# Turning x by a diagonal of reciprocal roots at the start of a gated hybrid attention layer

## What is computed

```python
def rmsnorm(x, g):
    xf = x.astype(jnp.float32)
    y = xf * lax.rsqrt(jnp.mean(xf * xf, axis=-1, keepdims=True) + RMS_EPS)
    return (y * g.astype(jnp.float32)).astype(x.dtype)

def hybrid_layer(x, norm_g, w_in, b_merge, w_pa, w_pb, w_out):
    h = rmsnorm(x, norm_g)
    proj = jnp.einsum('bsd,dc->bsc', h, w_in)
    # ... attention branches, gates and merge, all from proj
```

## Time and profile before

| | us |
|---|---|
| median of three runs | 443.52 (443.51 to 444.15) |
| profiled execution, its own time | 443.48 |
| its span, first to last instruction | 441.7 |
| TensorE busy | 431.6 (98%) |
| VectorE busy | 212.8 (48%) |
| ScalarE busy | 198.5 (45%) |
| GpSimd busy | 176.3 (40%) |

### The profile page before, as it was taken

One profiled execution on the slowest core, in us unless ns is written; L12 is line 12 of the kernel. 1 busy time (PEld: TensorE's weight loads), 2 busy tenths in 40 slices (PEclk: granted clock), 3 DMA queues, 4 the chain that ended last, 5 costly groups with the idle time before them and its releaser, 6 DMA issues.

```text
span 441.7 us, 6258 instructions
## 1 busy us (share of the span) xinstructions
PE 431.6 (98%) x2377; PEld 374.5 (85%) x2377; DVE 212.8 (48%) x367; ACT 198.5 (45%) x401; POOL 176.3 (40%) x113
## 2 busy tenths in 40 slices
PE   7899999999999999999999999999999999999995
PEld 6789998899889988988888888888888888888885
DVE  3831244344435446757857664827025173083334
ACT  5743555335544464567555554533223543332111
POOL 4744442243243333646499543534355354200000
PEclk9999999999999999999999999999999999999999
DMA  8962234622452263024122022222222284210421
GB/s 284 286 192 96 96 96 83 159 96 95 91 150 97 96 168 110 25 96 143 49 95 96 0 73 96 96 72 96 95 71 96 95 261 156 113 66 0 149 90 47
DMA packets 40044, 48.31 MB, mean 109 GB/s; under 512 B 3768, under 2 KB 35536, under 8 KB 40016
## 3 DMA queue, kind: packets, MB, share of 16 engines
q1 hardware_dynamic: 37568, 47.72, 34.4%
q10 hardware_dynamic: 2448, 0.21, 0.4%
HBM read 39.48 MB, written 2.15 MB: 94 GB/s over the span
## 4 chain that ended last, share of the span: by engine, by line
PE 96%; DMA 2%; DVE 1%; ACT 1%; SPq 0%; issue 0%; DVEq 0%; ACTq 0%
PE ps L766 20%; PE ps L770 20%; PE ps L767 20%; PE ps L816 4%; PE ps L818 4%; PE ps L817 4%; PE ps L890 3%; PE ps L974 3%; PE ps L975 3%; PE ps L973 3%; PE ps L873 3%; PE ps L917 3%; PE ps L907 2%; DMA xs<-in_x 2%; PE ps L865 1%; PE ps L850 0%
## 5 line engine op out<-in xcount | busy, mean ns | idle before, releaser
L662 POOL TENSOR_TENSOR w_lo<-raw,w_hi 128x1024 fp32r<-128x1024 f32 (+1 forms) x59 | 138.1, 2342 | 175.4 <-ACT w_hi L990 175.4
L766 PE MATMUL ps<-hT_hi,w_hi 128*128 128x512 f32 x336 | 135.0, 402 | 1.1 <-DVE hT_lo L1241 1.1
L770 PE MATMUL ps<-hT_lo,w_hi 128*128 128x512 f32 x336 | 131.2, 390 | 0.0
L767 PE MATMUL ps<-hT_hi,w_lo 128*128 128x512 f32 x336 | 131.1, 390 | 0.0
L770 PEld LDWEIGHTS ps<-hT_lo,w_hi 128*128 128x128 f32 x336 | 63.1, 188 | 13.5
L766 PEld LDWEIGHTS ps<-hT_hi,w_hi 128*128 128x128 f32 x336 | 63.2, 188 | 11.2 <-issue 1.3
L767 PEld LDWEIGHTS ps<-hT_hi,w_lo 128*128 128x128 f32 x336 | 63.3, 188 | 9.9
L990 ACT CAST w_hi<-raw 128x1024 fp32r<-128x1024 f32 (+1 forms) x58 | 59.2, 1020 | 8.3 <-PE ps L770 5.4
L816 PE MATMUL ps<-w_hi,hT_hi 128*128 128x256 f32 x160 | 45.6, 285 | 0.0
L818 PE MATMUL ps<-w_lo,hT_hi 128*128 128x256 f32 x160 | 44.7, 279 | 0.0
L817 PE MATMUL ps<-w_hi,hT_lo 128*128 128x256 f32 x160 | 44.6, 279 | 0.0
(11 more groups left out here) (148 smaller groups left out, 665.6 us busy)
## 6 DMA issues: line engine op xcount, KB each, us to landing
raw<-in_w_in SPq DMA_DIRECT2D x25, 1024.0 KB, 4.9
KTs<-KTs SPq DMA_DIRECT2D x20, 256.0 KB, 3.4
raw<-in_w_out SPq DMA_DIRECT2D x4, 1024.0 KB, 4.8
xs<-in_x SPq DMA_DIRECT2D x4, 512.0 KB, 5.3
raw<-in_w_pb SPq DMA_DIRECT2D x4, 512.0 KB, 4.1
res<-in_x SPq DMA_DIRECT2D x4, 512.0 KB, 3.9
out<-weighted SPq DMA_DIRECT2D x8, 256.0 KB, 2.1
raw<-in_w_in SPq DMA_DIRECT2D x2, 512.0 KB, 8.9
```

Of the source, the lines that this page charges most:

```text
L662: nc.gpsimd.tensor_tensor(ring(w_lo, n, kt), src, ring(w_hi, n, kt).bitcast(F32), ALU.subtract).then_inc(lo_ready, 1)
L766: pe.matmul(out, wh, hh, start=(k == 0), stop=False)
L767: pe.matmul(out, wl, hh, start=False, stop=False)
L770: return pe.matmul(out, wh, hl, start=False, stop=(k == kts - 1))
```

## The change

- x is not scaled any more. Per tile ScalarE squares the low half of the rows and VectorE the high half, VectorE makes `ss_mean`, ScalarE takes the root of both together (`rms`, kept in `var`), VectorE its reciprocal, and the identity times that reciprocal is a diagonal `diag[:, i, :]`. VectorE makes the diagonals of tiles 0 to 2, ScalarE that of tile 3.
- TensorE multiplies each block of x by the diagonal (`pe.matmul` with the block as the stationary operand), which turns and scales it at once. It was `pe.transpose` before.
- The vectors are turned right behind the warm-up, ahead of tile 0. VectorE copies them out behind tile 0's diagonal and ahead of tile 1's square.
- Of tile 2 six blocks are turned; the last two alternate with the first blocks of tile 3.
- The first half of the first weight chunk is loaded as two DMAs (k 0 to 3, k 4 to 7), with a semaphore each.
- POOL builds the distance tables behind the low part of step 2, and VectorE finishes the constants behind step 2's results.

```diff
 # sync
-                        sp.dma_start(dst[:, :, 0:P], w_in_t[:, :, at:at + P]).then_inc(first_half_in[0], 16)
-                        sp.dma_start(dst[:, :, P:256], w_in_t[:, :, at + P:at + 256]).then_inc(first_half_in[1], 16)
+                        for m, ks in enumerate((slice(0, FIRST_K), slice(FIRST_K, KT_D))):
+                            sp.dma_start(dst[:, ks, 0:P], w_in_t[:, ks, at:at + P]).then_inc(first_in[m], 16)
+                        sp.dma_start(dst[:, :, P:256], w_in_t[:, :, at + P:at + 256]).then_inc(first_in[2], 16)
 # gpsimd: iota and affine_select of d_full, d_band, d_quad, d_hex go into distances()
-            pool.wait_ge(first_half_in[0], 16)
+            pool.wait_ge(first_in[0], 16)
             nc.gpsimd.tensor_copy(hi[:, low_k, :], src[:, low_k, :]).then_inc(first_hi, 1)
+            pool.wait_ge(first_in[1], 16)
             nc.gpsimd.tensor_copy(hi[:, high_k, :], src[:, high_k, :]).then_inc(hi_ready, 1)
...
                 lows(n)
+                if n == CONST_STEP:
+                    distances()
 # tensor
-            for i in range(TT):
-                if i < HALVED:
-                    pe.wait_ge(x_scaled, i + 1)
-                else:
-                    pe.wait_ge(x_scaled_low, i - HALVED + 1)
...
-                    last = pe.transpose(ps[:, k, P * i:P * i + P], xs[:, i, P * k:P * k + P], ident[:, :])
...
+            pe.wait_ge(vec_in, 32)
+            pe.transpose(ps[:, 7, SEQ - 24:SEQ], vecs[:, :], ident[0:24, 0:24]).then_inc(vecs_turned, 1)
+            def scaled_turn(i, k):
+
+                return pe.matmul(ps[:, k, P * i:P * i + P], xs[:, i, P * k:P * k + P], diag[:, i, :],
+                                 start=True, stop=True)
+
+            for i in range(TT - 1):
+                pe.wait_ge(diag_ready, i + 1)
+                for k in range(KT_D if i < TT - 2 else FIRST_TURNS):
+                    if i == 0 and k == KT_D - 1:
+                        pe.wait_ge(gb_ready, 1)
+                    scaled_turn(i, k)
+            pe.wait_ge(last_diag, 1)
+            for k in range(KT_D):
+                scaled_turn(TT - 1, k).then_inc(x_turned, 1)
+                if FIRST_TURNS + k < KT_D:
+                    scaled_turn(TT - 2, FIRST_TURNS + k)
 # scalar
+            for i in range(TT):
+                low = slice(0, D // 2)
                 act.wait_ge(x_in[i], 16)
-                nc.scalar.activation(squares[:, i, 0:n], xs[:, i, 0:n], ACT.Square,
+                nc.scalar.activation(squares[:, i, low], xs[:, i, low], ACT.Square,
                                      accum_out=ss[:, i:i + 1]).then_inc(squared, 1)
...
+                act.wait_ge(squared, i + 1)
+                act.wait_ge(part_ready, i + 1)
+                nc.scalar.activation(var[:, i:i + 1], ss[:, i:i + 1], ACT.Sqrt, scale=1.0 / D,
+                                     bias=ss_mean[:, i:i + 1]).then_inc(rms_ready, 1)
+            act.wait_ge(last_root, 1)
+            nc.scalar.activation(diag[:, TT - 1, :], ident[:, :], ACT.Copy,
+                                 scale=rstd[:, TT - 1:TT]).then_inc(last_diag, 1)
 # vector
+            def square_rows(i):
+                high = slice(D // 2, D)
+                dve.wait_ge(x_in[i], 16)
+                link(nc.vector.scalar_tensor_tensor(out=squares[:, i, high], in0=xs[:, i, high], scalar=1.0,
+                                                    in1=xs[:, i, high], op0=ALU.mult, op1=ALU.mult,
+                                                    accum_out=ss_part[:, i:i + 1]))
+                nc.vector.tensor_scalar(ss_mean[:, i:i + 1], ss_part[:, i:i + 1], 1.0 / D, EPS, ALU.mult,
+                                        ALU.add).then_inc(part_ready, 1)
+
+            def root_diagonal(i):
+                dve.wait_ge(rms_ready, i + 1)
+                if i == TT - 1:
+                    nc.vector.reciprocal(rstd[:, i:i + 1], var[:, i:i + 1]).then_inc(last_root, 1)
+                    return
+                link(nc.vector.reciprocal(rstd[:, i:i + 1], var[:, i:i + 1]))
+                nc.vector.tensor_scalar(diag[:, i, :], ident[:, :], rstd[:, i:i + 1], None,
+                                        ALU.mult).then_inc(diag_ready, 1)
+
+            dve.wait_ge(consts_ready, 1)
+            for i in range(TT):
+                square_rows(i)
+                root_diagonal(i)
+                if i == 0:
+                    dve.wait_ge(vecs_turned, 1)
+                    link(nc.vector.tensor_copy(gb[:], ps[:, 7, SEQ - 24:SEQ]))
+                    nc.vector.tensor_scalar(hbias[:], gb[:, 8:24], 0.5, None, ALU.mult).then_inc(gb_ready, 1)
...
                 if s:
                     take_step(s - 1)
+                if s == CONST_STEP + 1:
+                    finish_constants()
```

More of the change, by code:

```diff
@@ L87 @@
 FIRST_K = 4
-HALVED = 2
+FIRST_TURNS = 6
 WARM = 14
 NRING = 4
+CONST_STEP = 2
 SKEW = 8
@@ L390, in hybrid_layer_program @@
         raw_in = [sem(f"raw_in{i}") for i in range(NRAW)]
-        first_half_in = [sem(f"first_half_in{i}") for i in range(2)]
+        first_in = [sem(f"first_in{i}") for i in range(3)]
         const_step = sem("const_step")
@@ L396, in hybrid_layer_program @@
         dve_chain = sem("dve_chain")
[L397 to L400, removed]
+        part_ready = sem("part_ready")
+        rms_ready = sem("rms_ready")
+        diag_ready = sem("diag_ready")
+        last_root = sem("last_root")
+        last_diag = sem("last_diag")
         first_hi = sem("first_hi")
@@ L738, in _ @@
                 pe.matmul(ps[:, 0, 0:P], ident[:, :], ident[:, :], start=True, stop=True)
-            for i in range(TT):
-                if i < HALVED:
-                    pe.wait_ge(x_scaled, i + 1)
-                else:
-                    pe.wait_ge(x_scaled_low, i - HALVED + 1)
-                for k in range(KT_D):
-                    if i >= HALVED and k == KT_D // 2:
-                        pe.wait_ge(x_scaled, i + 1)
-                    if i == 1 and k == 7:
-                        pe.wait_ge(gb_ready, 1)
-                    last = pe.transpose(ps[:, k, P * i:P * i + P], xs[:, i, P * k:P * k + P], ident[:, :])
-                    if i == TT - 1:
-                        last.then_inc(x_turned, 1)
-                if i == 0:
-                    pe.wait_ge(vec_in, 32)
-                    pe.transpose(ps[:, 7, SEQ - 24:SEQ], vecs[:, :], ident[0:24, 0:24]).then_inc(vecs_turned, 1)
+            pe.wait_ge(vec_in, 32)
[7 more added lines that the diff above has]
+                    if i == 0 and k == KT_D - 1:
+                        pe.wait_ge(gb_ready, 1)
+                    scaled_turn(i, k)
[4 more added lines that the diff above has]
+                    scaled_turn(TT - 2, FIRST_TURNS + k)
             def weights_wait(n):
@@ L1208, in turn_vectors @@
-            def turn_vectors():
-                dve.wait_ge(vecs_turned, 1)
-                link(nc.vector.tensor_copy(gb[:], ps[:, 7, SEQ - 24:SEQ]))
-                nc.vector.tensor_scalar(hbias[:], gb[:, 8:24], 0.5, None, ALU.mult).then_inc(gb_ready, 1)
-            for i in range(HALVED):
-                variance(i)
-                scale_rows(i, 0)
-            turn_vectors()
-            last, high = TT - 1, slice(D // 2, D)
-            dve.wait_ge(x_in[last], 16)
-            link(nc.vector.scalar_tensor_tensor(out=squares[:, last, high], in0=xs[:, last, high], scalar=1.0,
-                                                in1=xs[:, last, high], op0=ALU.mult, op1=ALU.mult,
-                                                accum_out=ss_part[:, 0:1]))
@@ L1230, in _ @@
-            nc.vector.reciprocal(rvar[:, last:TT], var[:, last:TT]).then_inc(var_ready, 1)
-            for i in range(HALVED, TT):
-                scale_rows(i, D // 2)
+            def square_rows(i):
[6 more added lines that the diff above has]
+                                        ALU.add).then_inc(part_ready, 1)
```

92 lines of the change are left out of this document (30 added, 62 removed).

## The result

The kernel after took 444.65 us (median of 20 executions, 443.40 to 446.99), the kernel before beside it 443.49 (20, 442.96 to 444.55). The ratio is 1.003, with an interval of 1.0019 to 1.0041: slower by 0.3%, where the forecast was 443.65 and no difference. 16 of the 20 lie between 443.4 and 445.1 and four between 446.7 and 447.0. The profiled execution is one of these four: 446.98 us, its span 445.1. The kernel before beside that second set has 443.54. So the medians differ by 1.2 and by 0.5 us, the two intervals together reach from a gain of 0.4 to a loss of 1.8 us, and the first set has a spread of 3.6 us that the prediction didn't expect. The question is what makes the start as long as 18 us, and what is there when it isn't.

The account below looks back on a forecast made before the run. TensorE was taken as the bound, busy 431.6 of 441.7 us, so the time shifts with the first projection matmul (14.58). 443.48 + 0.07 (diagonals and doubled turns) + 0.10 (POOL beside VectorE) = 443.65, range 442.9 to 444.3.

Parts of the forecast that it names:

- Part 2: VectorE's queue stands still until the vectors are turned behind the warm-up, at 6.98; tile 1's square then starts at 7.60.
- Parts 1 and 2: VectorE's queue before the first projection matmul: 1.51 us a tile, last diagonal seen by TensorE at 12.36.
- s1: Start of VectorE's square of tile 1, forecast at 7.60.
- s3: Start of VectorE's square of tile 3, forecast at 10.62.
- Part 4: POOL's first cast beside VectorE's square of tile 3: the square grows by 0 to 0.38, taken as +0.10 us.
- B: Rival: TensorE's clock rises later, so warm-up and tile 0's turns end later; together 444.5 us; chance 0.10.
- Rival A: VectorE's queue holds the tiles back less: 443.1 us, about 442.7 with the clock's rise 1 us earlier; chance 0.17.
- C: Rival: distance tables or constants aren't hidden; at twice their time step 3 waits 1.8 us: 445.4; chance 0.03.
- D: Rival: the last diagonal follows tile 3's landing and TensorE isn't in the way: 442.2 us; chance 0.05.
- The f32 turn as two instructions: TensorE's turns go from 0.11 to 0.224 us each, 32 from 3.6 to 7.2; first projection matmul at 14.65, +0.07.
- Part 5: Distance tables, constants and an additional load issue moved later on POOL, VectorE and SP: cost 0, bounds 0 and +0.3.

Follow-up runs that it names:

- second set: The changed kernel measured again, nothing altered, 12 executions: 444.05 us, ratio 1.0005 (0.9992 to 1.0018).
- r_after: The changed kernel run again unaltered, for a second profile: 444.05 us, ratio 1.0005, first projection matmul at 14.98.
- e4: The changed kernel with POOL's distance tables back in front of its first cast: 444.00 us, ratio 0.9999.
- e3: The changed kernel with the vectors turned behind tile 2's blocks, copied behind the low weights, and POOL's second cast waiting for VectorE's low weights: 445.24 us, ratio 1.0021.
- g1: The kernel before with only the split first weight load and the moved tables and constants; x still scaled and transposed: 444.37 us, ratio 1.0014.
- h3: The changed kernel with transposes by the identity instead of f32 matmuls by the diagonal, scaling of x left out: 444.18 us, ratio 1.0014.
- e2: The changed kernel with POOL waiting for VectorE's low weights before its second cast: 444.52 us, ratio 1.0005.
- h1: The changed kernel with the vectors turned after 9 of the 14 warm-up matmuls: 443.42 us, ratio 0.9994.
- e1: The changed kernel with the vectors turned behind tile 2's blocks and copied behind VectorE's low weights: 443.90 us, ratio 1.0006.
- f1: The changed kernel with 6 warm-up matmuls instead of 14: 443.82 us, ratio 1.0000.
- f2: The changed kernel with 6 warm-up matmuls instead of 14 and POOL's second cast waiting for VectorE's low weights: 443.85 us, ratio 1.0005.

## Why the prediction was wrong, step by step

The forecast had the first matmul at 14.58 + 0.07 + 0.10 = 14.75; the trace of 446.98 us has 18.00. The 3.25 us between them:

- **Part 2, when the queue moves on.** The forecast let the vectors' turn start at 6.98; it came at 7.59, 0.61 later, and at 6.34 in r_after. The mechanism was right, the moment was read from one trace of a quantity that varies: in the profiled executions of the same start the spacing of the instructions falls at moments between 4.6 (e4) and 7.3 (after, e3, g1, h3).
- **Parts 1 and 2, the length of a tile.** Forecast 1.51 us, measured 1.70 (7.92, 9.63, 11.33 in e2, with no long instruction). ScalarE's root with a tile as bias takes 0.30, not the 0.20 of the earlier trace rows. The diagonal takes 0.29, not 0.23: the row that I took it from multiplies by a constant. And the root starts 0.10 behind the mean, not 0.04. The two tiles between s1 and s3 make +0.39. Then the last tile: root +0.10, ScalarE's own diagonal 0.40 for 0.32 and somewhat longer gaps, +0.22 until TensorE has it. With the vectors' turn at the forecast's 6.98, e2's trace gives a first matmul at 15.61 - 0.37 = 15.24: 0.59 later than the forecast's 14.65 before its allowance for POOL. This term alone, put on the forecast, gives 444.24, between the two sets of after (444.05 and 444.65).
- **Part 4, POOL beside VectorE.** I took 0.10 with a bound of 0.38 on one instruction. Without contact and with its own turn of the vectors, after would have reached 15.61 + 0.24 = 15.85; it had 18.00, so contact cost 2.15, 2.05 more than the forecast's 0.10. Its parts are 0.41, 0.80 and 0.84 on three instructions in the chain, and 0.1 by the low weights, of which I had written that they hide, ending at most at 13.5; they ended at 17.08. The step that failed here is the form of the bound. I took the longest stretched instruction seen (1.07 against 0.69) as the worst a square can suffer. That row holds the answer, if POOL's is laid beside it: L1236 starts at 12.02, POOL's cast ends at 11.93 + 0.62 = 12.55, and L1236 ends at 13.09, 0.54 behind. It isn't a rate but a wait for the end of POOL's instruction, so its bound is the length of POOL's instruction (in this trace 1.27 for the product, and 2.67 for that of the next weights, which takes 2.40 undisturbed), for every VectorE instruction in the chain.

Sum: 0.61 + 0.59 + 2.05 = 3.25.

The median of the first set is another matter: 444.65 lies 1.00 above the forecast, and its first matmul would be near 15.7. Here the term that failed is the length of a tile, 1.70 for 1.51 and with the last tile 0.59 in all: the root and the diagonal were priced by rows without a tile as operand. The other 0.4 weren't taken apart. They are a later turn of the vectors or a meeting with POOL, or both; e2 without the meetings has nearly the same median (444.52), and h1 with the early copy has 443.42.

The Trainium skill (SBUF — State Buffer, "SBUF: two separate sides" and "Who interferes with whom") says this outright: VectorE and GpSimd share a pair of ports by an exclusive lock, held by whoever starts first for the whole instruction, and the other blocks fully; a VectorE instruction takes part if it runs in a two-port mode, or if it reads two SBUF inputs while GpSimd's instruction reads SBUF too. The traces here agree, in both directions: 1.52 against 0.68 where POOL was first, POOL's 1.72 against 1.27 where VectorE was. The prediction asked only who contends, and not in what form; by this rule the waits could have been bounded by POOL's own durations.

**The rivals.** B had the right direction, a late rise of the clock, with the wrong place and price: it was to decide from a rise at 9.0 and to give 444.5 at most. The trace of 446.98 us has its rise at 7.3. The price was counted as if only TensorE were slower; the delay goes into VectorE's queue first, and there meets POOL. The Trainium skill (TensorE: Matmul & The Clock Gate, Part 1, What you observe) gives 500 ns either way for the rise; two traces of the one kernel after have it at 4.7 and at 7.3, and the measurement decides. Rival A's early rise is in r_after (vectors at 6.34), but its first matmul is 14.98, where A's 443.1 needs one near 14.2: the longer tiles and one meeting with POOL (0.35) ate what it gave. C doesn't occur: no wait of TensorE behind the first matmul, and e4. D doesn't either.

**What was right.** The standstill behind the warm-up, with s1 0.58 behind the vectors' turn against a forecast of 0.62. The f32 turn as two instructions: 44 in a row take 5.08 us in e1, which is 43x0.112 and 0.27 for the last, and h3 shows that their doubling hides on this schedule. Part 5: the tables run on POOL behind step 2's low part and nothing waits.

```profile
24.29 0.57 POOL L683 IOTA d_full<- 128x512 f32 x1
...
28.61 0.24 POOL L700 IOTA d_hex<- 128x128 int32 x1
```

(That is POOL's timeline in the kernel after: 4.6 us, as forecast.) And from hT_hi to the first matmul it takes 1.73 to 1.76 us in all traces of the f32 turns but the one where the low weights end at 17.08 (1.81).

**What stays open.** Four of 20 executions of the first set lie at 446.7 to 447.0 and none of the 12 of the second. The one that was traced shows what such a time is made of. That the other three are the same is a reading of their times and of their mean granted clock (0.999 in all four), not shown. The kernel before has long executions too, four of the 35 beside e1 to e4 between 445.78 and 446.22, but of another kind: each has a mean granted clock of 0.991, as have the four over 445.8 in the other two sets of 35, and no execution of these sets with a higher one took over 444.82. None of them was traced; it looks like a fall of the clock, as in h3. So the prediction's remark against rival B, that 1.79 us of idle time didn't lower the clock, holds for the execution that was traced, and perhaps not for all. Nor is it shown that the whole 0.3% of the first set is the change's: the second set's interval holds 1.

## What to carry to other kernels

Before an instruction is put on a critical chain of VectorE, look at what POOL runs at that time: an instruction that reads two SBUF tiles, or an f32 tensor_scalar (here from 16 columns up, not with one), may wait for the end of POOL's, so let POOL's long ones wait for the chain or give VectorE a source in PSUM. Never put a small step that another engine must deliver (here: the copy of the vectors behind 14 warm-up matmuls) in an in-order queue ahead of the chain, unless its supplier is done earlier in the slowest execution too; asking for it in the middle of the warm-up cost nothing here (h1). And price an unseen operation by a row of the same operands (with a scale or bias from a tile the operations here took 0.06 to 0.10 us more than the rows with a constant), because a term of a tenth comes back once for each tile.

## What the runs showed of the hardware that was not expected

- A VectorE instruction of the kinds that follow, if it meets one of POOL's casts or products, doesn't end before that one does, whatever its own size: 128x512 with two inputs 0.68 to 2.05 us, 128x128 times a scalar 0.29 to 1.09, 128x16 times a constant 0.17 to 0.95, 128x1 with two inputs 0.16 to 0.56. The mean (128x1) and the reciprocal beside a running product keep their 0.15 and 0.17, and hT_lo, which has one operand in PSUM, its 0.74 or 0.75.
- It holds the other way too: POOL's 128x512 product takes 1.27 alone and 1.72 when VectorE's square started 0.09 us before it.
- The moment at which the spacing of f32 matmuls falls from 0.213 to 0.112 us (1.2 to 2.4 GHz) lies between 4.6 and 7.3 us in the twelve traces without f1 and f2, and at 8.8 in f1, where TensorE stood still from 4.5 to 5.2. The column of the granted clock shows 1.00 for such a start all the same, so the rise must be read from the spacing. The fall in h3 does show in the column (0.77, 0.61).
- The first weights land between 9.3 and 10.6 us in the kernels that load them in two pieces (POOL's first cast starts at 9.27 in r_after and at 10.62 in f1), over a microsecond apart, which decides as well whether POOL and VectorE meet: see h3.
